# A hybrid decoder layer on one core: prologue, weight sums, heads' norms and the way into the output projection rearranged

## The reference

```python
h = rmsnorm(x, norm_mix_g);  p = h @ w_in                # 2048 x 5120: u_A | v_A | B_gate | C_gate | x_B
u, v = gelu(u_A), rmsnorm(gelu(v_A), sgu_norm_g)
y_A = u * (tril(w_s[h]) @ v_chunk + b_s[h])              # 8 heads x 128 channels, chunks of 128 positions
y_B = B_gate * (b + sum_k w[k] * shift(C_gate * x_B, k)) # 8 groups x 128 channels, 3 taps
y = concat(group_rmsnorm(y_A, 8), group_rmsnorm(y_B, 8)) # a norm over each head's 128 channels
x = x + y @ w_out                                        # 2048 x 2048
h = rmsnorm(x, norm_ffn_g)
x = x + (silu(dwconv3(h @ w_gate)) * (h @ w_up)) @ w_down  # width 5632
return rmsnorm(x, final_norm_g)                          # and the last rows of both convolutions, and v
```

## Time and profile before

| what | value |
|---|---|
| median of 3 runs | 2316.51 us (2315.52 to 2318.67) |
| profiled execution, its own time | 2304.64 us |
| its span, first to last instruction | 2302.8 us |
| busy: PE, DVE, ACT, POOL | 96%, 77%, 48%, 28% of the span |
| mean granted clock of PE | 0.987 of full |

### The profile page before, as it was taken

The page is one execution under the profiler, slowest core; times in us unless marked ns, Lnnn a source line. Parts: engine busy times, 40 slices in busy tenths (PEclk is TensorE's granted clock), DMA queues, the critical chain, the costliest instruction groups (busy, mean ns, idle before and its releaser), DMA issues.

```text
span 2302.8 us, 43217 instructions
## 1 busy us (share of the span) xinstructions
PE 2222.2 (96%) x16584; PEld 2206.3 (96%) x16584; DVE 1765.3 (77%) x2315; ACT 1104.2 (48%) x1747; POOL 648.9 (28%) x730
## 2 busy tenths in 40 slices
PE   6999999998799999999999999999999999999997
PEld 5999999997799999999999999999999999999997
DVE  5677777776522598888888888888888898888886
ACT  6344443344211255445444444444544565555565
POOL 3330114443622111101111111111111355655573
PEclk9999999998899999999999999999999999999998
DMA  6444335546533334534444343444536666765433
GB/s 217 99 134 114 112 89 165 159 140 194 176 98 113 94 103 129 161 118 157 134 135 151 129 155 121 153 141 129 160 121 208 214 229 221 221 240 190 168 114 111
DMA packets 377576, 346.58 MB, mean 151 GB/s; under 512 B 10409, under 2 KB 350500, under 8 KB 372721
## 3 DMA queue, kind: packets, MB, share of 16 engines
q1 hardware_dynamic: 346608, 203.98, 30.5%
q0 software_dynamic: 30848, 140.99, 17.4%
HBM read 273.95 MB, written 70.97 MB: 150 GB/s over the span
## 4 chain that ended last, share of the span: by engine, by line
PE 60%; DMA 1%; DVE 1%; POOL 1%; issue 0%; ACT 0%; POOLq 0%; ACTq 0%
PE ps L2826 13%; PE ps L2828 13%; PE ps L2827 13%; PE ps L2887 6%; PE ps L2889 6%; PE ps L2888 6%; DMA form<-act_scratch 1%; PE ps L2901 0%; DVE w_lo L2183 0%; PE ps L2945 0%; PE ps L2947 0%; PE ps L2946 0%; POOL X L989 0%; POOL down L983 0%; POOL down_s L982 0%
## 5 line engine op out<-in xcount | busy, mean ns | idle before, releaser
L2887 PE MATMUL ps<-form,dw_hi 128*128 128x288 f32 x1204 | 356.8, 296 | 0.9 <-DMA form<-act_scratch 0.7
L2888 PE MATMUL ps<-form,dw_hi 128*128 128x288 f32 x1204 | 354.3, 294 | 0.0
L2889 PE MATMUL ps<-form,dw_lo 128*128 128x288 f32 x1204 | 353.7, 294 | 0.0
L2826 PE MATMUL ps<-hq,w_hi 128*128 128x288 f32 x1008 | 298.0, 296 | 1.1 <-DVE w_lo L2183 1.1
L2827 PE MATMUL ps<-hq,w_hi 128*128 128x288 f32 x1008 | 296.7, 294 | 0.0
L2828 PE MATMUL ps<-hq,w_lo 128*128 128x288 f32 x1008 | 296.1, 294 | 0.0
L2339 DVE TENSOR_TENSOR dw_lo<-down,dw_hi 128x512 fp32r<-128x512 f32 (+1 forms) x280 | 238.4, 857 | 72.4 <-ACT dw_hi L1085 71.9
L913 POOL DMA_DIRECT2D act_scratch<-stage x67 | 44.6, 666 | 657.4 <-DVE stage L2151 634.0
L2888 PEld LDWEIGHTS ps<-form,dw_hi 128*128 128x128 f32 x1204 | 227.5, 189 | 0.0
L2887 PEld LDWEIGHTS ps<-form,dw_hi 128*128 128x128 f32 x1204 | 225.7, 187 | 1.6 <-issue 1.6
L2889 PEld LDWEIGHTS ps<-form,dw_lo 128*128 128x128 f32 x1204 | 227.2, 189 | 0.0
(11 more groups left out here) (388 smaller groups left out, 6650.3 us busy)
## 6 DMA issues: line engine op xcount, KB each, us to landing
raw<-in_w_gate_dram SPq DMA_DIRECT2D x88, 512.0 KB, 4.3
down<-in_w_down_dram SPq DMA_DIRECT2D x32, 1024.0 KB, 5.5
form<-act_scratch POOLq DMA_DIRECT2D x28, 1152.0 KB, 7.1
act_scratch<-stage POOLq DMA_DIRECT2D x45, 576.0 KB, 4.7
raw<-in_w_in_dram SPq DMA_DIRECT2D x44, 512.0 KB, 5.1
raw_c<-in_w_up_dram SPq DMA_DIRECT2D x42, 512.0 KB, 3.8
raw_d<-in_w_up_dram SPq DMA_DIRECT2D x42, 512.0 KB, 5.0
raw<-in_w_out_dram SPq DMA_DIRECT2D x32, 512.0 KB, 4.0
```

What stands on the lines that cost most here:

```text
L2826: te.matmul(out, w_hi[:, c, j, :], b_form(t, 0, j), start=start and j == 0, stop=False, skip_group_check=True)
L2887: te.matmul(out, dw_hi[:, m % 4, j, :], act_f[:, j, 0, :], start=start and j == 0, stop=False, skip_group_check=True)
L2888: te.matmul(out, dw_hi[:, m % 4, j, :], act_f[:, j, 1, :], start=False, stop=False, skip_group_check=True)
L2889: last = te.matmul(out, dw_lo[:, m % 4, j, :], act_f[:, j, 0, :], start=False, stop=stop and j == n - 1, skip_group_check=True)
```

## The change

1. **Prologue.** ACT squares blocks 0 and 1 before any unit, block 2 after unit 1 of block 0, block 3 after unit 3 of block 2 and the last block after unit 1 of block 3; DVE builds the diagonals of blocks 1 and 2 after unit 0 of the block before. A root of one column is put early on ACT. 28 transposes of the identity stand on PE before the first block.
2. **Weight sums.** `sum1` is made from the loaded quarters alone and comes first, `sum3` is made from `sum2`'s result and comes after piece 2's split; the values are the same.
3. **Heads' norms.** `renorm` is one DVE instruction per head, put at 14 places in visits 9 to 17; POOL only loads and stores. Reciprocals and roots of the batches, and the sums of squares on PE, are at other places of the visits.
4. **Heads 14 and 15.** Their squares are summed against a full matrix of ones, so that each partition holds the sum; root and reciprocal are taken of 128 x 576, and nothing goes through DRAM.
5. **First pieces of w_out.** One piece has its own buffer (`raw_x`) and is loaded as soon as the last `x` tiles are used; the order of the loads and splits of the four first pieces is another.
6. **Residual.** DVE scales each tile of 576 columns just before it adds to it; POOL doesn't.

```diff
-    SKIP = 5 * WVIS
+    SKIP = 5 * WVIS + 2
-    BATCHES = ((0, HEADS), (HEADS, 4), (HEADS + 4, 2), (DIRECT, 2))
+    BATCHES = ((0, HEADS), (HEADS, 4), (HEADS + 4, 2))
+    WARM = 28
+        raw_x = sb("raw_x", [P, PK, P], at=u_at + 10368)
...
@@ sync @@
-            for tile in range(2):
-                sp.wait_ge(lo_ready, IN_PIECES - 2 if tile == 0 else IN_PIECES)
-                sp.dma_start(raw[:, tile], col(w_out, tile, 0)).then_inc(raw_landed[tile], 16)
-            for tile in range(2):
-                load(IN_PIECES + 2 + tile, tile, col(w_out, tile, 1))
+            sp.wait_ge(win_c21, WVIS - 1)
+            sp.wait_ge(z_ready, HEADS // 2)
+            sp.dma_start(raw_x[:, :, :], col(w_out, 0, 0)).then_inc(rawx_landed, 16)
+            sp.wait_ge(lo_ready, IN_PIECES - 2)
+            sp.dma_start(raw[:, 0], col(w_out, 1, 0)).then_inc(raw_landed[0], 16)
+            sp.wait_ge(lo_ready, IN_PIECES)
+            sp.dma_start(raw[:, 1], col(w_out, 0, 1)).then_inc(raw_landed[1], 16)
+            sp.wait_ge(lo_ready, IN_PIECES + 1)
+            sp.dma_start(raw_x[:, :, :], col(w_out, 1, 1)).then_inc(rawx_landed, 16)
@@ gpsimd @@
-            def renorm(k):
-                pool.wait_ge(yn_in, 32 * (k + 1))
-                g.tensor_scalar(ya[:, :], ya[:, :], vecs[:, G_OUT + k:G_OUT + k + 1], None, ALU.mult).then_inc(pool_scaled, 1)
-                pool.wait_ge(pool_scaled, 2 * k + 1)
-                g.tensor_tensor(ya[:, :], ya[:, :], ra[:, :], ALU.mult).then_inc(pool_scaled, 1)
-                pool.wait_ge(pool_scaled, 2 * k + 2)
+            def renorm_out(k):
+                pool.wait_ge(yn_done, k + 1)
                 g.dma_start(y_scr[:, k * T:(k + 1) * T], ya[:, :]).then_inc(yn_out, 16)
...
+            y_load(0, 0)
+            renorm_out(13)
+            y_load(0, 1)
...
+            y_load(1, 0)
+            y_load(1, 1)
...
-            resid_scale(0)
-            resid_load(2)
-            batch_out(3)
...
@@ scalar @@
+            a.activation(small[:, 23:24], eps_t, ACT.Sqrt)
...
             x_square(0)
+            x_square(1)
             for tb in range(TB + 1):
                 for kq in range(4):
                     x_unit(4 * tb + kq)
-                    if kq == 1 and tb < TB:
-                        x_square(tb + 1)
+                    if (tb, kq) in ((0, 1), (2, 3), (3, 1)):
+                        x_square({0: 2, 2: 3, 3: 4}[tb])
...
+            def last_root(n, dst, out, out_samp):
+                act.wait_ge(ssq_done, 1 + DIRECT + n + 1)
+                a.activation(dst[:, 0:SEQ], out, ACT.Sqrt, bias=eps_t, scale=1.0 / P)
+                a.activation(dst[:, SEQ:T], out_samp, ACT.Sqrt, bias=eps_t, scale=1.0 / P).then_inc(rms_ready, 1)
@@ vector @@
-                    if kq == 3 and tb < TB:
+                    if (tb, kq) in ((0, 0), (1, 0), (2, 3), (3, 3)):
                         x_diag(tb + 1)
             def sum3(vi):
                 dve.wait_ge(lo_ready, wq(vi, 0) + 1)
+                dve.wait_ge(sum_done, 4 * vi + 2)
+                v.tensor_tensor(raw[:, 0], a22(vi), win_c[:, :, :], ALU.subtract).then_inc(sum_done, 1)
...
             def sum2(vi):
                 dve.wait_ge(lo_ready, wq(vi, 1) + 1)
-                dve.wait_ge(sum_done, 4 * vi + 2)
-                v.tensor_tensor(win_c[:, :, :], a22(vi), raw[:, 0], ALU.subtract).then_inc(sum_done, 1)
+                dve.wait_ge(sum_done, 4 * vi + 1)
+                v.tensor_tensor(win_c[:, :, :], win_c[:, :, :], raw[:, 0], ALU.subtract).then_inc(sum_done, 1)
...
+            def renorm(k):
+                dve.wait_ge(yn_in, 32 * (k + 1))
+                v.scalar_tensor_tensor(out=ya[:, :], in0=ya[:, :], scalar=vecs[:, G_OUT + k:G_OUT + k + 1], in1=ra[:, :],
+                                       op0=ALU.mult, op1=ALU.mult).then_inc(yn_done, 1)
...
-                if vi == 16:
-                    batch_recip(2)
+                if vi == 17:
+                    renorm(13)
...
+                sum3(vi)
                 win_lo(vi, 3)
                 sum4(vi)
+                if vi == 9:
+                    batch_recip(0)
+                elif vi == 16:
+                    batch_recip(2)
+                elif vi in (10, 12, 15):
+                    renorm({10: 1, 12: 4, 15: 9}[vi])
...
                 win_lo(vi, 6)
-                if vi == 9:
-                    batch_recip(0)
+                if vi in (10, 11, 12, 13, 14, 15):
+                    renorm({10: 2, 11: 3, 12: 5, 13: 7, 14: 8, 15: 10}[vi])
...
                 if not last:
-                    sum1(vi + 1)
                     win_lo(vi + 1, 1)
+                if vi in (9, 12, 15):
+                    renorm({9: 0, 12: 6, 15: 11}[vi])
+                elif vi == 16:
+                    renorm(12)
...
+            def scale_resid(m):
+                xm = row(X, m)
+                v.tensor_tensor(xm, xm, rmsb[:, :], ALU.mult).then_inc(resid_scaled, 1)
             def w_out_tile(m, s, done=None):
+                scale_resid(m)
+                dve.wait_ge(resid_scaled, m + 1)
@@ tensor @@
+            for n in range(WARM):
+                te.transpose(ps[:, 0, 0:P], ident[:, :], ident[:, :])
...
+            def last_ssq(n, hi, lo, out, out_samp):
+                pe.wait_ge(ysqlo_ready, DIRECT + n + 1)
+                for dst, cols in ((out, slice(0, SEQ)), (out_samp, slice(SEQ, T))):
+                    te.matmul(dst, ones_r[:, :], hi[:, cols], start=True, stop=False, skip_group_check=True)
+                    last = te.matmul(dst, ones_r[:, :], lo[:, cols], start=False, stop=True, skip_group_check=True)
+                last.then_inc(ssq_done, 1)
-            out_by_k(0, range(0, 5))
-            y_ssq(DIRECT)
-            out_by_k(0, range(5, DIRECT))
+            out_by_k(0, range(0, 3))
+            pe.wait_ge(rms_ready, 1 + len(BATCHES))
+            last_ssq(0, sq_hi, sq_lo, ps[:, SSQ_BANK, :], ssq_samp)
+            out_by_k(0, range(3, 7))
+            last_ssq(1, sq15_hi, sq15_lo, ps[:, MIX_BANK, :], ps[:, T_BANK, 0:SAMP])
+            out_by_k(0, range(7, DIRECT))
```

More of the change, by code:

```diff
@@ L1322, in _ @@
                 win_hi(vi, 5)
+                if kind == "x" and vi > 6:
+                    y_square(win_head(vi - 1) + 1)
                 if mixing:
@@ L1375, in _ @@
+            for j in range(4, DIRECT // 2):
                 y_hi(1, j)
-            batch_root(3)
             split_hi(IN_PIECES + 4, 0, (piece_done, IN_PIECES + 1))
@@ L2034, in _ @@
                     win_lo(vi + 1, 0)
-                    sum3(vi + 1)
+                    sum1(vi + 1)
                 else:
@@ L2095, in _ @@
             w_out_tile(3, 1)
-            dve.wait_ge(pool_scaled, 2 * DIRECT + 4)
+            for s in range(1, 4):
+                dve.wait_ge(x_in[s], 2 * 16)
             with dve.Fori(2, KT // 2 - 1) as i:
@@ L2654, in _ @@
                 win_product(vi, 1, 2, True, False)
-                if kind == "x" and vi > 6:
-                    y_ssq(win_head(vi - 1))
                 if mixing:
@@ L2664, in _ @@
                     y_ssq(p0 - 1)
+                elif kind == "x" and vi > 6:
+                    y_ssq(win_head(vi - 1))
                 if mixing:
@@ L2669, in _ @@
                     v_transposes(p0 + 1)
-                elif kind == "x" and vi > 6:
-                    y_ssq(win_head(vi - 1) + 1)
                 elif vi == 2:
@@ L2679, in _ @@
                     mix(p0 + 1)
+                elif kind == "x" and vi > 6:
+                    y_ssq(win_head(vi - 1) + 1)
                 pe.wait_ge(p5_snap, vi + 1)
```

192 lines of the change are left out of this document (100 added, 92 removed).

## The result

| | median | runs | ratio to before, 95% interval |
|---|---|---|---|
| before | 2316.02 us | 4 (2306.07 to 2318.67) | |
| after | 2286.66 us | 4 (2282.18 to 2288.72) | 0.988 [0.985, 0.991] |

The change makes the kernel 29.4 us faster, where 39.4 us were forecast: 2286.7 for 2277.

A forecast was written before the change was run, and what follows sets the result against it. PE, busy 96% of the span, was taken as the bound, so gains come only from its waits and half clock. 6.6 + 7.8 + 3.0 + 22.0 = 39.4 us off 2316.5 gave 2277 us, range 2263 to 2294.

The forecast's parts named there:

- on the way into the output projection: Between visits and output projection: of 24.9 us of waits and clock 2.9 stay, so 22.0 us go; bounds 15 and 24.
- The heads' chain: Rival, heads 14 and 15: reciprocals on the path behind a late square, 9 us less gain, 2286; chance 0.09.
- The prologue: Before the first product: it starts at 39.0 us instead of 45.6, so 6.6 us go; bounds 3 to 9.
- takes the 5.2 of a block: Prologue: the last full block starts at 33.8 us and takes 5.2, so the first product starts at 39.0.
- so that the whole moves along: Behind the prologue: engines feeding PE wait for PE or one another, so its gain of 6.6 us carries on.
- Visits 0 to 8: Early visits: sum1 comes 1.6 us earlier and sum2 behind it, so 7.8 us go; bounds 3 and 8.3.
- sum3 stands ahead of piece 3's split, where 1.2 of the 1.6 gained is given back: Visits 0 to 8: sum3 ahead of that split returns 1.2 of the 1.6 us gained.
- Visits 9 to 17: Later visits: of 18.5 us of waits and clock 15.5 stay, so 3.0 us go; bounds 8 lost and 14 gained.
- 1.2 x 4: Visits 9 to 17: 1.2 us of wait at each of four norms standing some 7 us behind the one before.
- DVE's waits take the visits' gain: Rival: visits 9 to 17 lose 8 us instead of gaining 3, total gain 24 us, 2292; chance 0.23.
- Everything hides: Rival, whole kernel: loads land in 4 us and DVE has the lead, gain 55.3 us, 2261; chance 0.15.
- The slower case: Rival, norms' waits on DVE: slower than before from 39.4 us of further PE waits, 2326 at 49 us; chance 0.04.

The follow-up runs named there:

- e12: The changed kernel unaltered, measured again beside the last follow-up kernels: 2287.99 us, ratio 0.989 to the kernel before.
- e1: The changed kernel unaltered, measured once more beside the first follow-up kernels: 2286.35 us, ratio 0.989 to the kernel before.
- e2: The changed kernel with only the prologue put back as it was (squares, diagonals, early root, no transposes of the identity): 2289.23 us, ratio 0.991.
- e7: The changed kernel with sum3 of each visit moved behind the low part of the fourth piece: 2291.35 us, ratio 0.992.
- e3: The changed kernel with only the weight sums back in the old order (sum3, sum1, sum2, sum4): 2296.31 us, ratio 0.993.
- e4: The changed kernel with the 14 norms on DVE left out, so those heads stay unnormalized: 2269.7 us, ratio 0.982.
- e5: The changed kernel with nine of the norms at later places, further apart, same work and transfers: 2277.37 us, ratio 0.987.
- e6: The changed kernel with block 3's square and diagonal two units earlier in the prologue: 2288.38 us, ratio 0.991.
- e9: The changed kernel with a second set of later norm places and sum3 behind the fourth piece in visit 0 alone: 2281.65 us, ratio 0.988.
- e11: The changed kernel without the 28 transposes of the identity at PE's start (WARM = 0): 2286.25 us.

## Why the prediction was right or wrong, by its steps

**The direction and the bulk were right.** Most of the gain is where it was put, on the way into the output projection: 22.0 forecast, 19.8, 20.9 and 20.3 measured. Both long waits are gone, the reciprocals and roots run while PE works: the last of the two multiplications is at 579.02 and no wait follows. Against the 2.3 us of waits that were kept for it stand 2.8 for squares (0.67 and 2.12). Behind them PE works at half clock in after and e12 (0.83 in 560 to 570 us, 1.7 us lost where 0.6 were put); in e1 the clock stays at 1.00 and the stretch is 1.1 us short of the forecast. The heads' chain, a rival, was hidden, as the forecast had it.

**The prologue: right in its chain, 0.6 to 1.6 us short of the sum.** Diagonal 3 stood at 33.97 where 33.8 was worked out, from block 1 landed at 9.2 and the table load at 3.19. What failed is the next term, "takes the 5.2 of a block": PE had stood still for 8.91 us before it, and the block took 6.3 us (5.5 in e1). The 5.2 was read as a block at full clock, and it wasn't: the records of that block in before start 0.21 us apart for the first 14 and 0.11 apart for the other 18, those of block 3 after 0.21 apart for the first 27 (19 in e1). The gap was in the sum's own plan (ACT squares block 3 behind all units of block 2), and its clock wasn't charged. The same reading hid what a slow start costs: the "1.3 us" between two blocks of before is the difference of two that both began at half, not the whole price. A second thing failed, "so that the whole moves along": 3.1 us behind the first products went to a half-clock stretch in some executions, in which PE had not waited, and e2 shows no gain of the prologue at the down projection.

**Visits 0 to 8: 4.6, 4.4 and 6.2 instead of 7.8.** The step that failed is "sum3 stands ahead of piece 3's split, where 1.2 of the 1.6 gained is given back" with 0.5 left. It is the last sum in DVE's row that now makes piece 3 late: 0.92, 0.71 and 0.34 us in visits 1 to 3, and 2.42 in visit 0, where the first form of the input is made as well and where 0.93 more stand ahead of it. e7 took some of them away, got a new one, and lost more later, so the order chosen is the better of the two; e3 shows the term's sign and gives 3.6.

**Visits 9 to 17: the mis-sized term.** Forecast 15.5 us left of 18.5. Against e4's 195.7 us, whose PE waits 1.0 for pieces, the changed kernel's 216.4 has 21 to 22 us of waits and clock, and before's 213.5 has 18 to 19. So what was there before was counted right, and what would be left was too little by 6. By the traces of before and after, PE's waits in the stretch are 13.2 and 15.4 us, and the half-clock stretches cost 5.1 and 4.6 (their length less PE's idle time in it, halved); 1.3 us of the rest are neither. The forecast's 15.5 was 13.8 of waits and 1.7 of clock: so it had the waits 1.6 too small and the clock 2.9. Two parts of it:
- "1.2 x 4" for norms 7 us apart was near in its sum (4.5 us at those four heads) and wrong in its places. At heads 1, 5 and 10 DVE stood still 1.11, 3.35 and 3.74 us and PE 0, 0 and 0.64. At head 2 in visit 10 DVE stood still 6.79 us and PE 3.88, and heads 6 and 11, which weren't counted, stopped DVE for 1.81 and 2.33, with waits of PE of 1.18 and 1.69 behind them. Head 2's loads, issued from 367.93 on, landed at 375.3, 6.8 us after the second was issued, where the earlier trace rows has 3.7. SP had issued three quarters of weights at 365.90, 367.04 and 368.54, in front of and beside them; that they are the cause is likely and not shown. I had used one head's landing and the mean of fourteen for the distance that decides; the slowest of the fourteen takes 7.1 us, and the trace of before has seven of fourteen at 5.1 to 6.4.
- One half-clock stretch was counted, at 1.7 us, and there were two, behind the waits of 3.88 and 4.53. PE's waits here are 15.3 us (the rows for visits, 300 to 560 us: 10.5, 3.9 and 0.9); the two stretches cost some 2.4 and 2.2 us. The count went by a reading of before, a stretch behind each wait of 2.0 us or more in the visits; after and e12 have a wait of 2.42 us without one.

```profile
375.30 0.82 DVE L1901 SCALAR_TENSOR_TENSOR ya<-ya,vecs,ra 128x576 f32<-128x576 f32 x1 [6.79 <-DMA ra<-r_scratch]
376.54 0.61 PE L2688 MATMUL ps<-t4f,w_hi 128*128 128x288 f32 x1 [3.88 <-DVE half_sum L1976]
```

The largest single one, head 13 in visit 17, was forecast as 4.0 and measured 4.53, and the norm waited for the reason given: POOL waited 3.92 us for the store of the head before rather than 2.11, with its load behind it.

**The rivals.** "DVE's waits take the visits' gain" is what happened in kind: visits 9 to 17 lost 2.3 to 3.9 rather than gaining 3.0. It was priced at 8 lost and 2292, and the 2286.7 measured is nearer to it than to the forecast of 2277. It lies just over the 2268 to 2286 that was given to the forecast itself, and within the whole range because that reaches on towards this rival: the sum of 39.4 us was 10 too large. e4 shows it by taking the norms away, e5 by moving them: a third to a half of the cost is the place, not the work. "Everything hides" needed 12 to 13 far apart and failed there as said. The slower case would have needed 39.4 us more of waits, and the norms cost 20 to 22 in all.

**The port.** The prediction worked out by the Trainium skill (SBUF — State Buffer, Who interferes with whom) 46 us more for DVE from the residual's scaling, with a meeting of DVE and POOL in every tile, and left its sum as it was. That was right: the stretch that holds most of the output projection is 1166.1 us long before and after. But the trace doesn't speak against the page, for the meetings are few. The 16 instructions took 12.9 us, a median of 750 ns each, and 13 of them ran while POOL did no such work, in most tiles because its square started some 1 us behind their end. One, the second of the two in the second row below, started while POOL's square ran, which ended at 747.69, and ended itself at 748.31: it took 1704 ns. Before, the multiplication of 5.73 us in the earlier trace rows ran from 598.23 to 603.96 beside POOL's scaling of the residual, which ended at 603.33, and the same operation behind it, with no such work beside it, took 0.81. Both agree with the page's exclusive lock.

```profile
593.30 10.03 POOL L865 TENSOR_TENSOR X<-X,rmsb 128x2304 f32<-128x2304 f32 x2
```

```profile
745.93 2.37 DVE L2126 TENSOR_TENSOR X<-X,rmsb 128x576 f32<-128x576 f32 x2
```

```profile
746.17 1.52 POOL L880 TENSOR_TENSOR psq<-X 128x576 f32<-128x576 f32 x1 [9.67 <-DVE X L2135]
```

**The own time.** The forecast was tied to the median of before, since the profiled execution lay 11.9 us under it. Of the two that was the better choice: its down projection is 8 us shorter than those of the changed kernel's three profiles. That the slower executions of before have the longer one is likely and not shown, for none was profiled. The later medians of before, 2308.6 to 2312.2, lie 4 to 8 us over that execution.

## What to carry to other kernels

An operation moved to an engine that works in order can cost more than its length, since all behind it waits with it: 11.4 us of norms cost 20 to 22 where they stood (16.7 by the medians of the whole), and 7 to 12 of these went by giving each norm a place about one full round trip (store, load, landing, 9 us here) behind the one before. Take the slowest landing of the trace for such a distance, above all next to a burst of weight loads, and charge each new gap of several us with a stretch at half clock: one followed each of the waits of 3.9 and 4.5 us in after, while behind the same wait of 2.42 us in visit 0 the clock fell in e1 and not in after and e12. Before a block's time is used as its time at full clock, look at how far apart its records start. A move that takes one short wait away can open a longer one elsewhere (e7, e6, e9), so each is to be timed alone and together.

## What the runs showed of the hardware that I had not expected

- The clock fell to half for 6.8 us (0.53 and 0.79 in two windows of 5 us) while PE was busy without a break, in two of the three profiles of the changed kernel: 24 instructions in 50 to 55 us against 39 in e1. What decides it is open.
- The column of the granted clock doesn't show all of a slow start. In 10 to 15 us it says 1.00 both for after and for e11 (and for before, whose first block starts as slowly as e11's), but PE makes 46 instructions in one and 31 in the other, and until 13.57 us those of e11 start 0.21 us apart instead of 0.11:

```profile
10.00:15.00 5.00, 5.00 (x46) 4.87 (x44) 4.06 (x8) 4.82 (x8) 1.54 (x2) 1.00 1.14 321
```

```profile
10.00:15.00 5.00, 5.00 (x31) 5.00 (x31) 2.87 (x7) 3.74 (x8) 0.79 (x1) 1.00 1.15 329
```
- A load of 128 x 576 by POOL's queue landed 3.3 to 7.1 us after its issue (median 3.9), in one kernel and one execution; in before it was 3.4 to 6.4 (median 4.4).
